# A decoder trunk with routed experts: router and shared gate as one product, choice of experts tile by tile, gate parts on GpSimd, and seventeen zero products at the start

## The chip, the core and the metric

The kernel runs on one core of a Trainium2 chip. The core has five engines with queues of their own: TensorE (PE, matrix products into the eight PSUM banks), VectorE (DVE), ScalarE (ACT), GpSimd (POOL, which works in SBUF) and SyncE (SP, which here issues nearly all DMA transfers). They wait for each other through semaphores. The metric is the device time of one execution in microseconds, lower is better.

## The reference

Two layers of a decoder on 256 tokens of 1024 values. In each, attention heads and four memory heads run side by side, one output projection and a layer norm follow, then a mixture of experts and a second norm. Everything is float32. What the change touches is the head of the mixture:

```
aff = jax.nn.sigmoid((xt @ w_router).astype(jnp.float32))          # 64 experts
sel = aff + router_bias
gscore = jnp.sum(lax.top_k(sel.reshape(n, 8, 8), 2)[0], axis=-1)    # 8 groups of 8
gidx = lax.top_k(gscore, 4)[1]
emask = jnp.repeat(gmask, 8, axis=1)
eidx = lax.top_k(jnp.where(emask, sel, -jnp.inf), 8)[1]
gates = jnp.take_along_axis(aff, eidx, axis=-1)
gates = gates / jnp.sum(gates, axis=-1, keepdims=True) * 2.5
...
h = jax.nn.silu(xb @ w_gate[e]) * (xb @ w_up[e]);  yb = h @ w_down[e]
shared = (jax.nn.silu(xt @ ws_gate) * (xt @ ws_up)) @ ws_down
```

Every expert has matrices of 1024x256, 1024x256 and 256x1024 (1 MB each), so the two layers read some 400 MB of expert weights.

## The kernel before

**Tiles.** The 256 tokens are two tiles of 128 (`t`). Products over the 1024 columns run over eight parts `k` of 128. A float32 product is two PE instructions in the trace, called rows below, so a product of one tile over eight parts is 16 rows. Weights stream from HBM through `ring`, twelve places of one matrix each; `first_place` says where the matrices of the dense part lie, `before_it` which load has to wait for which matrix in the same place. Some first expert weights are prefetched during the dense part, in the order that the SP block writes out.

**Start.** `warm(WARM)` multiplies zeros into bank 7 (L790, nine times) until the transposed input and the first half of the key weights are there; the first real product is L888.

**From the output projection to the experts**, per layer, in PE's order: the last rows of the projection (L869); the logits of tile 0 (L811, 64 columns a row); the shared expert's gate product of tile 0 (L1126, 256 columns), interrupted by products of zeros that open the output sums (L1153) and by the transposes of tile 1 (L800), which need its norm (DVE L1686 to L1693); logits of tile 1; the shared expert's other products; the rank product (place of each token within its expert, and counts), which waits for `chosen`; twelve more rows of the shared expert; then the gather of the tokens of eight experts into `xg` (L811, 32 rows), the first turn-back (L1222, with the product of the one-hot tile and `gparts`, the gates split into three bf16 parts) and the first gate product of the expert loop (L1250). The loop goes over 32 pairs of experts: gate (L1250), up (L1269), down (L1303), and scatter into the sums (L1311).

**DVE** in this stretch: norm of tile 1, two copies of its transpose to `xT`, then the choice for both tiles at once (L1853 to L1886: sigmoid's end, maxima of each group, comparison of the groups, eight best), `chosen`; the shared hidden product (L1891) of tile 0; rank, counts and the one-hot of eight experts (L1902); gates and their three parts (L1928 to L1939), with the shared hidden product of tile 1 among them; then copies of the gathered chunks. **ACT** takes square roots, makes the float32r copy of x (`x_high`), copies xT of tile 0, exponentiates the logits (L1567) and applies Silu to the shared gate products (L1570). **POOL** makes the low part of x of tile 1 (L774). **SP** issues weight loads, each behind a wait for the work that frees the place.

## Time and profile before

| | us |
|---|---|
| median of 3 runs | 1195.70 |
| the three runs | 1195.63, 1195.70, 1197.05 |
| the profiled execution, its own time | 1196.97 |
| its span from the first to the last instruction | 1195.2 |
| PE busy | 1154.6 (97%) |
| DVE, ACT, POOL busy | 345.4, 299.2, 54.9 |
| read from HBM | 445.91 MB |

The profile is of one execution. Times within it count from the start of the span. A view of lines tells the duration of one instruction, which for PE overlaps its neighbours; the chain of work tells start to start, so that a number of rows divided into it gives the pace. Busy slices and DMA shares are parts of each slice.

### The profile page before, as it was taken

How to read it: one execution, taken by the hardware profiler on the slowest of the kernel's cores; microseconds unless marked ns; L12 is line 12 of the kernel's file. 1: busy time of each engine (PE TensorE's matmuls, PEld its weight loads, DVE VectorE, ACT ScalarE, POOL GpSimd, SP SyncE). 2: the span in 40 equal slices, each digit the busy share in tenths (PEclk: the TensorE clock that was granted, in tenths of full speed). 3: DMA queues.
4: the chain of work that ended last, by engine and by line, in shares of the span. 5: the costliest groups of instructions: out<-in, count | busy, mean ns of one | idle time of the engine just before them, and what ended most of it. 6: DMA issues, size and time to landing. Idle time of an engine off the chain costs nothing.

```text
span 1195.2 us, 22277 instructions
## 1 busy us (share of the span) xinstructions
PE 1154.6 (97%) x8905; PEld 699.6 (59%) x8907; DVE 345.4 (29%) x900; ACT 299.2 (25%) x709; POOL 54.9 (5%) x90
## 2 busy tenths in 40 slices
PE   8999999999999999999999999999999999999995
PEld 6875755555555555554787658555555555555542
DVE  0335512222122212221523556122222222122214
ACT  1354212222122212121214523122221212122212
POOL 1341000000001000000011000000000010000000
PEclk9999999999999999999999999999999999999998
DMA  9944899999999999999980558999999999999994
GB/s 373 408 163 154 308 418 420 427 429 428 428 427 427 400 428 428 428 427 425 414 337 1 235 228 342 417 412 429 429 426 428 429 416 384 414 427 429 429 427 193
DMA packets 38374, 447.96 MB, mean 375 GB/s; under 512 B 4256, under 2 KB 4640, under 8 KB 9120
## 3 DMA queue, kind: packets, MB, share of 16 engines
q1 hardware_dynamic: 37584, 442.25, 88.8%
q10 hardware_dynamic: 720, 4.73, 1.0%
q8 instruction: 50, 0.82, 0.3%
q14 instruction: 20, 0.16, 0.0%
HBM read 445.91 MB, written 1.05 MB: 374 GB/s over the span
## 4 chain that ended last, share of the span: by engine, by line
PE 88%; DMA 8%; DVE 2%; issue 1%; ACT 1%; DVEq 0%; SPq 0%; ACTq 0%
PE bank L1250 18%; PE bank L1269 17%; PE bank L1303 17%; PE bank L811 8%; PE bank L830 8%; PE bank L1311 5%; PE bank L869 4%; DMA ring<-in_w_gate 4%; DMA ring<-in_w_down 3%; PE bank L1126 2%; PE bank L1276 2%; PE bank L845 1%; PE bank L1149 1%; PE bank L1025 1%; PE bank L888 1%
## 5 line engine op out<-in xcount | busy, mean ns | idle before, releaser
L1269 PE MATMUL bank<-ring,work 128*64 128x256 f32 x1952 | 225.0, 380 | 10.3 <-issue 10.3
L1250 PE MATMUL bank<-ring,work 128*64 128x256 f32 x1984 | 227.8, 382 | 4.9 <-DMA ring<-in_w_gate 4.7
L1303 PE MATMUL bank<-ring,work 128*32 128x512 f32 x1904 | 222.1, 595 | 0.2
L1250 PEld LDWEIGHTS bank<-ring,work 128*64 128x64 f32 x1984 | 137.9, 137 | 116.2 <-issue 41.9
L1269 PEld LDWEIGHTS bank<-ring,work 128*64 128x64 f32 x1952 | 145.1, 137 | 79.4 <-issue 14.7
L1965 DVE SCALAR_TENSOR_TENSOR yhalf<-bank,gcol,yhalf 128x512 fp32r<-128x512 f32 x124 | 93.1, 751 | 214.2 <-ACT yhalf L1591 214.2
L1591 ACT ACTIVATE yhalf<-bank,gcol 128x512 fp32r<-128x512 f32 x124 | 85.2, 687 | 181.3 <-PE bank L1303 181.3
L1957 DVE TENSOR_TENSOR work<-work,bank 128x256 f32<-128x256 f32 x64 | 26.9, 421 | 357.5 <-PE bank L1269 357.5
L1303 PEld LDWEIGHTS bank<-ring,work 128*32 128x32 f32 x1904 | 57.1, 110 | 117.2 <-issue 109.2
L1433 ACT ACTIVATE work<-bank 128x512 f32<-128x512 f32 (+4 forms) x177 | 77.9, 440 | 100.5 <-PE bank L811 41.8
L1433 ACT ACTIVATE back<-bank 128x128 fp32r<-128x128 bf16 x64 | 17.7, 277 | 276.2 <-PE bank L1222 276.2
L830 PE MATMUL bank<-xT,ring 128*128 128x256 f32 x352 | 77.7, 380 | 0.0
L811 PE MATMUL bank<-hot,xhalf 128*128 128x256 f32 x512 | 72.8, 293 | 4.7 <-DVE work L1672 4.3
L1311 PE MATMUL bank<-yhalf,back 64*128 64x512 f32 x504 | 75.7, 418 | 0.0
L1672 DVE COPY work<-bank 128x512 f32<-128x512 f32 (+3 forms) x77 | 51.3, 670 | 82.1 <-PE bank L811 48.8
L1581 ACT ACTIVATE work<-bank 128x256 f32<-128x256 f32 x64 | 24.6, 384 | 192.4 <-PE bank L1250 192.4
L830 PEld LDWEIGHTS bank<-xT,ring 128*128 128x128 f32 x352 | 66.3, 190 | 9.3 <-issue 0.7
L811 PEld LDWEIGHTS bank<-hot,xhalf 128*128 128x128 f32 x512 | 64.9, 190 | 10.7 <-DVE work L1672 7.2
L1311 PEld LDWEIGHTS bank<-yhalf,back 64*128 64x128 f32 x504 | 42.5, 185 | 30.1 <-issue 23.8
L869 PE MATMUL bank<-ring,work 128*128 128x512 f32 x128 | 57.8, 594 | 0.0
L869 PEld LDWEIGHTS bank<-ring,work 128*128 128x128 f32 x128 | 23.2, 190 | 23.3 <-issue 23.0
L782 POOL TENSOR_TENSOR x<-xhalf 128x1024 f32<-128x1024 f32 x4 | 9.5, 2414 | 510.9 <-PE bank L1303 510.9
(186 smaller groups left out, 825.3 us busy)
## 6 DMA issues: line engine op xcount, KB each, us to landing
ring<-in_w_gate SPq DMA_DIRECT2D x62, 2048.0 KB, 15.3
ring<-in_w_down SPq DMA_DIRECT2D x56, 2048.0 KB, 16.3
ring<-in_w_up SPq DMA_DIRECT2D x56, 2048.0 KB, 17.1
ring<-in_w_up SPq DMA_DIRECT2D x10, 1024.0 KB, 6.8
ring<-in_w_in_b SPq DMA_DIRECT2D x3, 3072.0 KB, 19.7
ring<-in_w_out SPq DMA_DIRECT2D x4, 2048.0 KB, 12.4
ring<-in_w_down SPq DMA_DIRECT2D x7, 1024.0 KB, 10.4
home<-in_w_gate SPq DMA_DIRECT2D x4, 1024.0 KB, 16.2
```

Source lines behind the costliest of these rows:

```text
L811: last = pe.matmul(dst, a, b, start=(n == 0), stop=(n == len(pairs) - 1))
L830: mm = pe.matmul(bank_at(g)[:, c * 256:(c + 1) * 256], w[:, k, c0 + c * P:c0 + (c + 1) * P], moving[:, k, :], start=(k == 0), stop=(k == K ...
L869: last = pe.matmul(bank_at(g)[:], mixT[:, c, t * P:(t + 1) * P], item_view((l, f"out{half}"), 512)[:, c, :], start=start, stop=(done == KT))
L1250: last = pe.matmul(gate_bank[slots_of(e), 0:HID], xg[:, k, slots_of(2 * j + e)], w[e][:, k, :], start=(k == 0), stop=(k == KT - 1))
L1269: last = pe.matmul(up_bank[slots_of(e), 0:HID], xg[:, k, slots_of(2 * j + e)], w[e][:, k, :], start=(k == 0), stop=(k == KT - 1))
L1303: last = pe.matmul(yb[half][rows_of(t, e), :], hT[b][:, f, slots_of(e, t)], w[e][:, f, half * 512:half * 512 + 512], start=(f == 0), stop= ...
L1311: pe.matmul(sums[2 * t + half][:], back[b][rows_of(t), :], yhalf[rows_of(t), n, half * 512:half * 512 + 512], start=False, stop=False)
L1433: return act.activation(dst, src, ACT.Copy)
L1591: act.activation(yhalf[:, 0, half * 512:half * 512 + 512], yb[half][:], ACT.Copy, scale=gcol[:, j:j + 1])\
L1672: return dve.tensor_copy(dst, src)
L1957: dve.tensor_tensor(hidrow, sg, up_bank[:, 0:HID], ALU.mult).then_inc(s_("h_ready"), 1)
L1965: dve.scalar_tensor_tensor(out=yhalf[:, 1, part], in0=yb[half][:], scalar=gcol[:, j:j + 1], in1=yhalf[:, 0, part].bitcast(F32), op0=ALU.mu ...
```

## The change

- `wr`, the router's weights, moves in front of the ring (`store` holds both), and the shared gate's weights are laid out on the host in four column blocks of 64, at ring place 0. So router and shared gate form one moving operand of 5 x 64 = 320 columns, `router_gate[:, :, k, :]`. For each tile one product of 320 columns (`logits_and_gate`) goes to one bank (3 for tile 0, 0 for tile 1). In layer 0 the shared weights swap their places and their turn in the loads with `out1`, as layer 1 had it.
- DVE chooses per tile (`choose(t)`), on 64 columns; the groups are masked by one addition instead of a product and an addition. ACT makes an exponential per tile and copies the second half of tile 1's xT.
- DVE makes the gate sums and their reciprocals; POOL scales the gates and splits them into the three parts (six steps, each waited for). PE waits for these steps through the semaphore `const`.
- The shared hidden product of tile 1 stands ahead of the gate sums. The gather's second and third chunk wait for one shared hidden product each.
- `WARM` is 17 instead of 9.

```
-         ("xr1", "DD", (0, 1)), ("logit", "A", (2,)), ("rank", "D", (2,))],
+         ("logit0", "A", (3,)), ("xr1", "DA", (0, 1)), ("logit1", "A", (0,)), ("rank", "D", (3,))],
...
-        {"in1": 0, "in0": 3, "memkv": 6, "out0": 8, "shared": 3, "out1": 0},
+        {"in1": 0, "in0": 3, "memkv": 6, "out0": 8, "out1": 3, "shared": 0},
...
-        ring = sb("ring", [P, 2 * REGION * MATRIX])
+        store = sb("store", [P, KT * NE + 2 * REGION * MATRIX])
+        wr = store[:, 0:KT * NE].rearrange("p (k n) -> p k n", k=KT)
+        ring = store[:, KT * NE:]
+        router_gate = store[:, 0:KT * (NE + HID)].rearrange("p (c k n) -> p c k n", k=KT, n=NE)
...
-        shared_gu = ((banks[3][:, 0:HID], banks[3][:, HID:2 * HID]), (banks[0][:, 0:HID], banks[1][:, 0:HID]))
+        shared_gate = (banks[3][:, NE:NE + HID], banks[0][:, NE:NE + HID])
+        shared_up = (banks[2][:, 0:HID], banks[1][:, 0:HID])
...
-        WARM = 9
+        WARM = 17
...
                 used(sp, (l, "out1"))
-                if l == 0:
-                    pair(0, 0, 1, 0)
-                else:
-                    expert(1, 0, 3, 1)
-                    expert(1, 0, 2, 2)
+                expert(l, 0, 3, 1)
+                expert(l, 0, 2, 2)
...
                 used(sp, (l, "shared"))
-                if l == 0:
-                    expert(0, 0, 3, 1)
-                    expert(0, 0, 2, 2)
-                else:
-                    pair(1, 0, 1, 0)
+                pair(l, 0, 1, 0)
...
+                pool.wait_ge(sem(f"gate_sums_{l}"), 1)
+                for t in range(TT):
+                    step(pool.tensor_scalar(gate[:, t, :], gate[:, t, :], grec[:, t:t + 1], None, ALU.mult))
+                gp = [gparts[:, :, :, i] for i in range(3)]
+                step(pool.tensor_copy(gp[0], gate[:]))
+                step(pool.tensor_tensor(gate[:], gate[:], gp[0], ALU.subtract))
+                step(pool.tensor_copy(gp[1], gate[:]))
+                step(pool.tensor_tensor(gp[2], gate[:], gp[1], ALU.subtract))
...
+                def logits_and_gate(t):
+
+                    g = G[l, f"logit{t}"]
+                    dst = bank_at(g)[:, 0:NE + HID].rearrange("p (c n) -> p c n", n=NE)
+                    bank_free(pe, g)
+                    for k in range(KT):
+                        if k % 4 == 0:
+                            evacuated(pe, G[l, f"xr{t}"] + k // 4)
+                        last = pe.matmul(dst, xT[:, k, t * P:(t + 1) * P], router_gate[:, :, k, :], start=(k == 0), stop=(k == KT - 1))
+                    last.then_inc(sem("group"), 1)
...
-                pe.wait_ge(sem("chosen"), l + 1)
+                pe.wait_ge(sem("chosen"), TT * (l + 1))
                 g = G[l, "rank"]
                 bank_free(pe, g)
-                bank = bank_at(g)
+                pe.wait_ge(sem(f"shared_silu_{l}"), 1)
...
-                        if backs is None and k == 2:
-                            pe.wait_ge(sem(f"shared_h_{l}"), TT)
+                        if backs is None and k in (1, 2):
+                            pe.wait_ge(sem(f"shared_h_{l}"), k)
...
-                    pe.wait_ge(s_("gates_set"), 1)
+                    pe.wait_ge(sem("const"), CONSTS + (GATE_STEPS + 1) * l + GATE_STEPS)
...
                 norm_std(2 * l, 1)
+                logit_exp(0)
+                turned_x(1, 1)
                 x_high(1)
-                g = G[l, "logit"]
-                filled(act, g)
-                act.activation(rsc[:], bank_of(g, TT, NE), ACT.Exp, scale=-1.0).then_inc(read, 1)
+                logit_exp(1)
...
+                def choose(t):
...
+                    link(dve.tensor_reduce(grank[:, t, :], cmp1[:, t], AX_X, ALU.add))
+                    link(dve.tensor_scalar(goff[:, t, :], grank[:, t, :], float(TOPK_GROUPS), -BIG, ALU.is_ge, ALU.mult))
+                    grouped = sel[:, t, :].rearrange("p (g e) -> p g e", g=NGROUP)
+                    link(dve.tensor_tensor(grouped, grouped, to_rows(goff[:, t, :], PER_GROUP), ALU.add))
+                    link(dve.max(top8[:, t, :], sel[:, t, :]))
+                    link(dve.match_replace(rsc[:, t, :], top8[:, t, :], sel[:, t, :], -2.0 * BIG))
+                    dve.tensor_tensor(chosen[:, t, :], rsc[:, t, :], sel[:, t, :], ALU.not_equal).then_inc(sem("chosen"), 1)
...
+                shared_hidden(1)
                 link(dve.tensor_tensor(gate[:], aff[:], chosen[:], ALU.mult))
                 link(dve.tensor_reduce(gsum[:], gate[:], AX_X, ALU.add))
-                link(dve.reciprocal(grec[:], gsum[:]))
-                for t in range(TT):
-                    last = dve.tensor_scalar(gate[:, t, :], gate[:, t, :], grec[:, t:t + 1], ROUTED_SCALE, ALU.mult, ALU.mult)
-                shared_hidden(1)
-                link(last)
-                gp = [gparts[:, :, :, i] for i in range(3)]
-                link(copy(gp[0], gate[:]))
-                link(dve.tensor_tensor(gate[:], gate[:], gp[0], ALU.subtract))
-                link(copy(gp[1], gate[:]))
-                dve.tensor_tensor(gp[2], gate[:], gp[1], ALU.subtract).then_inc(s_("gates_set"), 1)
+                link(dve.tensor_scalar(gsum[:], gsum[:], 1.0 / ROUTED_SCALE, None, ALU.mult))
+                dve.reciprocal(grec[:], gsum[:]).then_inc(sem(f"gate_sums_{l}"), 1)
```

PE's instructions in layer 0 from the end of the output projection on, before (a program's product counts once here; `ident` is the identity for transposes, `zeros` the products that open sums):

```order
L869 MATMUL bank5<-ring,work 128x512 x2
L811 MATMUL bank2<-wr,xT 128x64 x8
L1126 MATMUL bank3<-ring,xT 128x256 x6
L1153 MATMUL bank4<-zeros 128x512
L1153 MATMUL bank6<-zeros 128x512
L800 MATMUL bank0<-ident,x 128x128 x4
L800 MATMUL bank1<-ident,x 128x128 x4
L1126 MATMUL bank3<-ring,xT 128x256 x2
L1153 MATMUL bank5<-zeros 128x512
L1153 MATMUL bank7<-zeros 128x512
L811 MATMUL bank2<-wr,xT 128x64 x8
L1126 MATMUL bank3<-ring,xT 128x256 x8
```

The same place in the change:

```order
L872 MATMUL bank5<-store,work 128x512 x2
L1141 MATMUL bank3<-store,xT 128x320 x8
L1162 MATMUL bank4<-zeros 128x512
L1162 MATMUL bank6<-zeros 128x512
L803 MATMUL bank0<-ident,x 128x128 x4
L803 MATMUL bank1<-ident,x 128x128 x4
L1162 MATMUL bank5<-zeros 128x512
L1162 MATMUL bank7<-zeros 128x512
L1141 MATMUL bank0<-store,xT 128x320 x8
L1129 MATMUL bank2<-store,xT 128x256 x8
L1129 MATMUL bank1<-store,xT 128x256 x2
L814 MATMUL bank3<-chosen,before 128x128
```

Nothing of the gate product is left behind the transposes of tile 1, and ten products of the shared up matrix stand ahead of the rank product.

DVE before, from the one-hot of the first eight experts to the last gate part (`route` holds gates and affinities, `work` the shared hidden values):

```order
L1902 TENSOR_TENSOR hot8_51<-slot_no,rank 128x512
L1927 TENSOR_LOAD nround_i
L1927 ISA x2
L1928 TENSOR_TENSOR route<-route,chosen 128x128
L1929 TENSOR_REDUCE gsum<-route 128x2
L1930 RECIPROCAL grec<-gsum 128x2
L1932 TENSOR_SCALAR route<-route,grec 128x64 x2
L1891 TENSOR_TENSOR work<-work,bank1 128x256
L1672 CAST gparts<-route 128x128
L1937 TENSOR_TENSOR route<-route,gparts 128x128
L1672 CAST gparts<-route 128x128
L1939 TENSOR_TENSOR gparts<-route,gparts 128x128
```

DVE in the change, from the same one-hot:

```order
L1905 TENSOR_TENSOR hot8_51<-slot_no,rank 128x512
L1932 TENSOR_LOAD nround_i
L1932 ISA x2
L1894 TENSOR_TENSOR work<-work,bank1 128x256
L1934 TENSOR_TENSOR route<-route,chosen 128x128
L1935 TENSOR_REDUCE gsum<-route 128x2
L1936 TENSOR_SCALAR gsum<-gsum 128x2
L1937 RECIPROCAL grec<-gsum 128x2
```

And POOL in the change, between the low part of x and its next wait for the loop:

```order
L769 TENSOR_TENSOR xhalf<-x,xhalf 128x1024
L773 TENSOR_SCALAR route<-route,grec 128x64 x2
L775 CAST gparts<-route 128x128
L776 TENSOR_TENSOR route<-route,gparts 128x128
L777 CAST gparts<-route 128x128
L778 TENSOR_TENSOR gparts<-route,gparts 128x128
```

The six steps behind the reciprocal have gone from DVE to POOL, and the shared hidden product has gone ahead of the gate sums.

## Rows read from the trace of the kernel before

**Rows 1.** The page, busy totals and DMA share in 40 slices:

```profile
PE 1154.6 (97%) x8905; PEld 699.6 (59%) x8907; DVE 345.4 (29%) x900; ACT 299.2 (25%) x709; POOL 54.9 (5%) x90
...
DMA  9944899999999999999980558999999999999994
```

**Rows 2.** Waits of PE: line, releaser, total us, times, longest:

```profile
PE bank L1269 <- issue: 10.3, 8, 1.3
PE bank L1250 <- DMA ring<-in_w_gate: 4.7, 6, 0.9
```

**Rows 3.** Chain of work, layer 0: start, us, what:

```profile
114.38 1.73 PE bank L811 x16
...
123.14 7.83 PE bank L1126 x36
130.97 0.13 PE bank L811 x2
...
138.61 3.67 PE bank L1250 x32
```

**Rows 4.** Timeline of PE, layer 0, with idle time before in brackets:

```profile
135.03 3.19 PE L811 MATMUL bank<-hot,xhalf 128*128 128x256 f32 x24 [0.21 <-DVE work L1891]
138.37 0.17 PE L811 MATMUL bank<-gparts,hot_tile 128*128 128x12 bf16 x1 [0.15 <-issue]
```

**Rows 5.** Chain of work, layer 1:

```profile
715.45 1.73 PE bank L811 x16
...
739.44 3.67 PE bank L1250 x32
```

**Rows 6.** Stretch 132:134 (last columns: clock, DMA share, GB/s), and SP's issues:

```profile
132.00:134.00 2.00, 2.00 (x11) 1.56 (x11) 1.54 (x6) 0.00 (x0) 0.00 (x0) 1.00 0.00 0
...
133.76 0.33 SPq L448 DMA_DIRECT2D ring<-in_w_up  x1
...
142.31 0.33 SPq L455 DMA_DIRECT2D ring<-in_w_gate  x1
```

**Rows 7.** Start: timeline, then L888 by starting time (ns min/median/max, first to last start):

```profile
1.26 4.02 PE L790 MATMUL bank<-zeros 128*128 128x512 bf16 x9 [1.26 <-DVE zeros L1699]
7.24 10.44 PE L888 MATMUL bank<-xT,ring 128*128 128x256 f32 x32 [1.96 <-DMA ring<-in_w_in_a]
10.13 0.33 SPq L423 DMA_DIRECT2D ring<-in_w_in_a  x1
...
L888 PE MATMUL bank<-xT,ring x4: 633/634/688, 10.9 to 12.3; 128*64 128x256 f32 x4
...
L888 PE MATMUL bank<-xT,ring x6: 379/380/483, 13.5 to 14.8; 128*128 128x256 f32 x5, 128*64 128x256 f32 x1
```

**Rows 8.** Timeline of DVE, layer 0, from the norm to the choice:

```profile
117.63 1.28 DVE L1693 SCALAR_TENSOR_TENSOR x<-x,rstd,lnrow 128x1024 f32<-128x1024 f32 x1
...
123.57 0.49 DVE L1853 TENSOR_SCALAR route<-route 128x128 f32<-128x128 f32 x1 [2.46 <-ACT route L1567]
...
125.08 0.29 DVE L1855 TENSOR_TENSOR route<-route,biasrow 128x128 f32<-128x128 f32 x1
125.41 1.19 DVE L1859 MAX8 top<-route 128x8 f32<-128x8 f32 x16
...
130.32 0.29 DVE L1886 TENSOR_TENSOR chosen<-route 128x128 bf16<-128x128 f32 x1
```

**Rows 9.** POOL's groups by form (busy us, mean ns), then its timeline:

```profile
L770 POOL TENSOR_SCALAR soft<-acc,rden 128x256 f32<-128x256 f32 x18 | 16.4, 923 | 47.6 <-DVE rden L1781 47.6
L770 POOL TENSOR_SCALAR soft<-acc,rden 128x128 f32<-128x128 f32 x12 | 7.2, 602 | 34.6 <-DVE rden L1781 34.6
L774 POOL TENSOR_TENSOR xhalf<-x,xhalf 128x1024 fp32r<-128x1024 f32 x2 | 5.7, 2846 | 115.4 <-ACT xhalf L1433 115.4
...
1.60 0.29 POOL L709 CAST ident_bf<-ident 128x128 bf16<-128x128 f32 x1
1.95 0.20 POOL L710 MEMSET ones<- 128x128 bf16 x1
```

More of the change, by code:

```diff
@@ L1880, in _ @@
[L1880 to L1886 removed]
+                    link(last)
+                    link(dve.tensor_tensor(gsc[:, t, :], top2[:, t, :, 0], top2[:, t, :, 1], ALU.add))
```

130 lines of the change are left out of this document (55 added, 75 removed).

## The prediction

> **What bounds the kernel now.** I read the page's totals and slices first. TensorE (PE) is busy 97% of the span, and the DMA engines stand at nine or ten tenths in most slices [rows 1]. So two resources are near their limit, and the question for each stage is which waits for which. The table of waits answers it: over 1195 us PE waited only 4.7 us for expert weights and 10.3 us for "issue" inside L1269, in stretches of 1.3 us at most [rows 2]. Apart from that PE simply works from one instruction to the next.
>
> The stretch that the change rewrites runs, in layer 0, from the end of the output projection at 114.38, where the logits begin, to the first gate product of the experts at 138.61. The chain of work is there PE all the way down to the rank product at 130.97 [rows 3], and in those 24.23 us PE idled 0.21 us ahead of the gather's third chunk and 0.15 ahead of the first turn-back [rows 4]. Layer 1 takes 739.44 - 715.45 = 23.99 us [rows 5]. So time taken off PE here is time off the path, as long as the helpers keep up.
>
> Does a shorter stretch shorten the expert loop, where DMA runs at its limit? The DMA share is 0.00 from 132 to 134: the queue was empty, because SP waited for the shared expert's products before it could issue at 133.76, and for the first expert gate product before it issued at 142.31 [rows 6]. Both releases come from PE. Whatever PE gains before them, the weight stream starts that much earlier, and the loop, paced by that stream or by PE, moves as a block.
>
> At the start there are nine products of zeros from 1.26 us, and the first real product (L888) starts at 7.24, when its weights have landed. Its 32 instructions take 10.44 us. Those that start up to 12.3 us last 634 ns, those after 13.5 us 379 [rows 7]. At one level of the clock (2.4 GHz) 32 instructions at 0.215 us would take 6.9 us. The excess is 3.5 us, of which some 2.8 are clock: from 7.24 to about 12.85 PE ran at the lower level (1.2 GHz), and half of those 5.6 us is lost. The granted-clock column itself says 1.00 there; the durations are what I go by.
>
> **The change part by part.**
>
> (a) *One product of 320 columns.* Before, each tile costs 16 rows of 64 columns (1.73 us, 0.108 each) and 16 rows of 256 (36 rows in 7.83, so 0.215 without the joints) [rows 3]. 64 columns are a quarter of 256 but cost half: the stationary load sets the pace. In the change a row has 320 columns: 0.215 x 320/256 = 0.269, so 4.30 us a tile against 1.73 + 3.44 = 5.17. That is 0.87 us a tile, 1.74 a layer, all of it on the path.
>
> (b) *The new order on PE*, layer 0, from 114.38: product of tile 0 to 118.68; two zero products (0.43) to 119.11. The transposes of tile 1 need the second norm, which ends at 117.63 + 1.28 = 118.91 [rows 8], so they don't wait. Transposes 0.93 to 120.04 and zeros to 120.47. The first half of xT is copied by DVE as before (0.65 us after its half, 120.3); the second half is now ScalarE's (ACT), one copy of 0.55 by about 120.7, needed only at the fifth row. Tile 1 to 124.77. Twenty rows of the shared up product to 129.07.
>
> (c) *Choice tile by tile.* Before, DVE chose for both tiles from 123.57 to 130.61 (7.04 us), and PE got to the rank product at 130.97: hidden by 0.36 us [rows 3, 8]. In the change each operation is half as wide. A 128-wide one lasts 0.29 us and 0.04 to the next; of that about half is independent of the width, so 64 columns take 0.22. The reciprocal (the 1.0 us between the first step and 125.08) and the maxima (sixteen in 1.19) halve; one step of two is gone where the group mask was made and applied. Going through the list: about 4.5 us a tile, 9.0 in all against 7.04. But tile 0 can start early: its logits are ready at 118.68, ACT's exponential at 119.0, and DVE is free behind its copy at about 120.7. So tile 0 ends at 125.2; tile 1's exponential is out at 125.1; tile 1 ends at 129.7. PE, there at 129.07, waits 0.65 us. Queued behind that wait are the rank product, 12 up rows and the gather. The bounds: no wait, if each step costs 8% less; 1.5 us, if halving the width saved nothing outside the two large steps.
>
> (d) *From the rank product to the gates.* Rank product to 129.86; 12 up rows (2.58) to 132.44; DVE's path from the rank product to the one-hot isn't touched; before, it was done while PE worked off those 12 rows, and it still is. Gather 32 rows at 0.133 (24 rows in 3.19 [rows 4]) to 136.69. The shared hidden product of tile 1 now stands ahead of the gate sums, and waits for the up rows (132.5 to 133.0); the third chunk of the gather needs it at 133.5. No wait, where there were 0.21 us before.
>
> (e) *Gate parts on GpSimd (POOL).* DVE is left with a product, a sum (0.33 each), a scaling and a reciprocal of two columns (0.2 each): 1.0 us, done at 134.0. Then six steps on POOL, each waited for: two scalings 128x64, two casts and two subtractions 128x128. POOL's scaling lasts 602 ns at 128 columns and 923 at 256, so 2.5 ns a column and 0.44 us at 64; a cast of 128x128 lasted 290 ns, and the next step began 0.06 later; a 1024-wide subtraction 2846 ns, from which I take 0.55 us at 128 [rows 9]. Sum 0.88 + 0.59 + 1.10 + 6 x 0.07 = 3.0 us, so the parts are ready at 137.05. On DVE the same steps ended at 136.2, and nobody waited. PE needs them at 136.69 for the first turn-back: it waits 0.35 us. Behind that wait stands the whole expert loop. With 0.24 us for turning back, the first gate product starts at 137.3 instead of 138.61. **Gain 1.3 us a layer, 2.6 us for both.** Bounds: 1.8 a layer if neither wait (c) nor (e) appears; nothing if POOL needs 4.3 us (rows of 0.65 on average: the 128-wide scaling is already 0.60).
>
> The Trainium skill, GPSIMD Engine Reference, section 4.1 Engine selection, tells to keep elementwise work on VectorE: about twice as slow on GpSimd with two inputs, about equal with one. The trace has one input at 2.5 ns a column on POOL, so it doesn't bear out the "equal". By the page's ratios, applied to DVE's rows, the six steps would take an estimated 2.8 us, 0.2 less than my sum.
>
> (f) *ACT and POOL moved.* The exponential and the half copy of xT go ahead of ACT's copy of x for tile 1, which could start at 118.9 and now starts at 120.7; POOL's low part (2.85 us [rows 9]) ends at 125.7 instead of 124.0. The gather needs it at 132.4, SP's load into x waits for it: 1 MB issued 1.7 us later while 2 MB are under way. Hidden; if that cover were gone it would cost 1.7 us of DMA.
>
> (g) *Layer 0's loads.* out1 and the shared weights change places and order. The bytes are the same. The second pair's gate weights now wait for the shared products; issued at 132.5 into an empty queue, some 7 us before they have landed, they are needed after the gate and up products of the first pair, at about 145. Zero; layer 1 has this order already, and its whole stretch is the shorter one.
>
> (h) *Seventeen zero products.* At the lower level each takes 0.427 us (nine in 4.02 with the last one's tail [rows 7]), so they'd end at 1.26 + 17 x 0.427 = 8.5, 1.3 us after the real product could start. If the clock rises while they run, they end earlier and the real product finds 2.4 GHz. In the trace it rose after 5.6 us of unbroken work. The same after 1.26 is 6.9: 13 zeros slow, 4 fast, PE free at 7.75, 0.5 late. Gain 2.8 - 0.5 = **2.3 us**. The second half of the weights isn't in the way: SP saw it landed at 10.13 [rows 7], and it is wanted at 11.2. Bounds: 2.8 (the rise comes early enough) and -1.3 (zeros leave the clock low). The dense part behind it never waits for data, so this is carried to the end.
>
> **Sum.** The profiled execution took 1196.97 (span 1195.2 and 1.8 around it): 1196.97 - 2.6 - 2.3 = 1192.1. It is 1.3 us above the median of 1195.7; the runs fall at 1195.6, 1195.7 and 1197.05. If that 1.3 is the moment when the clock rises, a typical run has less to win at the start, and 1192 stays; if it is elsewhere, 1190.8. I say **1191.4**.
>
> **The rivals.** *No wait at all* (the choice and POOL both faster than I sized them): 2 x 1.8 + 2.8 = 6.4 off, less half of the 1.3: 1189.9. For it: each wait is a few tenths. *POOL sets the gates*: the interleaved bf16 writes cost more than any POOL row shows, six steps take 4.3 us, routing gains nothing: 1194.0. *The weight stream hides it*: PE comes earlier to the experts but the bytes set the end; then only part of (h) survives, 1194.5. Against it stands the empty queue [rows 6]. *Zeros don't lift the clock*: +1.3 - 2.6 gives 1195.0; for it speaks that nine zeros (4 us) were followed by a slow product. *Slower than before*, by the same place as the second: from 5.5 us for POOL's six steps on, the kernel loses more at both turn-backs than it wins elsewhere; at 7.5 us (1.6 us for each of the four 128-wide steps) each layer starts its experts 3.1 us later than now, +6.3 - 2.3: about 1199. No row of POOL is near that: 7.5 us is 2.5 times my sum.
>
> **Chances.** Forecast 0.55, no waits 0.13, POOL sets the gates 0.13, weight stream 0.05, zeros without effect 0.10, slower 0.04. A measurement of this kernel can tell about 0.2% (2.4 us) from no change, so faster means under 1193.3: forecast and no waits, and a part of the second and third: 0.78. Same 0.18, slower 0.04. The range takes in the bounds of (c), (e) and (h) down to 1189.0 and reaches to the POOL and stream cases up to 1194.6.
>
> **What would show it.** L888 at 379 ns from its first instruction, starting at 7.2 to 7.8 (else (h) fails). The 320-column rows 0.27 apart; if they are 0.32 (the sum of the two old rows), (a) gives nothing. PE's wait for `chosen` 0 to 1.5 us. POOL's six steps 3 us, ending within 0.5 of the gather's end. First gate product of layer 0 at 137.3 less the gain of the start, and the same shift still there at the last product. If the shift at the first gate product is right and missing at the end, the weight stream was the bound.

## The result, and the profile of the changed kernel

The changed kernel takes 1197.65 us (median of 20 runs, 1196.03 to 1200.59) against 1196.05 for the kernel before, run beside it (20 runs, 1194.73 to 1197.87). The ratio is 1.0015, with a 95% interval of 1.001 to 1.0021: slightly slower, where 1191.4 was forecast. The profiled execution took 1200.59 (span 1198.9), 3.6 us more than the profiled execution of before. The totals and the DMA shares of the page stand nearly where they stood in [rows 1]:

```profile
PE 1153.4 (96%) x8849; PEld 695.0 (58%) x8851; DVE 349.0 (29%) x908; ACT 300.2 (25%) x713; POOL 60.2 (5%) x102
...
DMA  9935799999999999999970657999999999999995
```

So the time moved inside stretches. I read them in the order of the prediction. The start, from the timeline of PE (start, us, what; idle time before it in brackets), against [rows 7]:

```profile
1.26 5.33 PE L793 MATMUL bank<-zeros 128*128 128x512 bf16 x17 [1.26 <-DVE zeros L1707]
7.56 4.68 PE L891 MATMUL bank<-xT,store 128*128 128x256 f32 x19 [0.97 <-DMA store<-in_w_in_a]
```

And the same line's instructions by their durations (ns min/median/max, first to last start):

```profile
L891 PE MATMUL bank<-xT,store x32: 379/379/483, 7.6 to 14.8; 128*128 128x256 f32 x16, 128*64 128x256 f32 x16
```

All 32 real products run at 379 ns, the higher level of the clock (2.4 GHz), from the first one on. The output projection ends at 111.88 instead of 114.38: 2.5 us won. Then layer 0's stretch, again PE's timeline, with the weight loads (PEld) of the second wide product as its first row, against [rows 3, 4]:

```profile
118.03 4.07 PEld L1141 LDWEIGHTS bank<-store,xT 128*128 128x128 f32 x16 [0.46 <-DVE xT L1680]
118.06 4.54 PE L1141 MATMUL bank<-store,xT 128*128 128x320 f32 x16
122.44 4.48 PE L1129 MATMUL bank<-store,xT 128*128 128x256 f32 x20
129.28 0.22 PE L814 MATMUL bank<-chosen,before 128*128 128x128 bf16 x1 [2.36 <-issue]
...
129.39 4.25 PE L1129 MATMUL bank<-store,xT 128*128 128x256 f32 x12
133.08 4.60 PE L814 MATMUL bank<-hot,xhalf 128*128 128x256 f32 x32
138.54 0.17 PE L814 MATMUL bank<-gparts,hot_tile 128*128 128x12 bf16 x1 [0.87 <-DVE work L1680]
...
138.78 1.52 PE L1254 MATMUL bank<-store,work 128*64 128x256 f32 x12
```

PE stands idle for 2.36 us ahead of the rank product, the twelve up rows behind it need 4.25 us, and there is a second wait of 0.87 ahead of the turn-back. In the chain of work the wide product of tile 0 takes 4.31 us and that of tile 1 4.54: its first weight load waited 0.46 us for DVE's copy of xT. The first gate product starts at 138.78, where it started at 138.61: all that the start had won is gone. From 111.88 the stretch takes 26.90 us instead of 24.23. Layer 1, from the chain of work, against [rows 5]:

```profile
716.24 4.31 PE bank L1141 x16
...
726.97 4.32 PE bank L1129 x20
733.64 0.27 PE bank L814 x2
733.91 4.27 PE bank L1129 x12
...
743.07 0.17 PE bank L814
```

With the turning back behind the last row (0.24 us, as in layer 0) that is 743.31 - 716.24 = 27.07 us instead of 23.99. The account from trace to trace: start -2.5, layer 0 +2.67, between the stretches +0.6, layer 1 +3.08, the rest -0.2; together +3.7, which is the difference of the spans.

Why is the choice late? The timelines of DVE (the first three rows) and of POOL (the others), layer 0:

```profile
120.28 0.23 DVE L1878 TENSOR_TENSOR cmp<-cmp,lower 128x64 f32<-128x64 f32 x1
120.54 2.75 DVE L1879 TENSOR_TENSOR cmp<-cmp 128x64 f32<-128x64 f32 x1
123.33 0.22 DVE L1880 TENSOR_REDUCE grank<-cmp 128x8 f32<-128x64 f32 x1
```

```profile
120.30 2.92 POOL L769 TENSOR_TENSOR xhalf<-x,xhalf 128x1024 fp32r<-128x1024 f32 x1 [27.60 <-ACT xhalf L1437]
135.20 0.98 POOL L773 TENSOR_SCALAR route<-route,grec 128x64 f32<-128x64 f32 x2 [11.98 <-DVE grec L1937]
...
137.73 0.46 POOL L778 TENSOR_TENSOR gparts<-route,gparts 128x128 bf16<-128x128 f32 x1
```

One comparison (L1879, an addition of two 64-wide inputs) lasts 2.75 us, its neighbours 0.22. It ends at 123.29, and POOL's low part of x ends at 123.22. In layer 1 the same line lasts 2.76 us. Nothing in the two instructions depends on the other. And the clock, from the table of stretches (busy us of PE, PEld, DVE, ACT, POOL, then granted clock, DMA share, GB/s):

```profile
126.00:128.00 2.00, 0.92 (x5) 0.47 (x3) 1.79 (x15) 0.00 (x0) 0.00 (x0) 1.00 0.74 311
128.00:130.00 2.00, 0.72 (x5) 0.70 (x6) 1.79 (x9) 0.00 (x0) 0.00 (x0) 1.00 0.00 0
130.00:132.00 2.00, 2.00 (x8) 1.66 (x7) 1.42 (x7) 0.00 (x0) 0.00 (x0) 0.65 0.00 0
132.00:134.00 2.00, 2.00 (x7) 1.64 (x7) 0.25 (x1) 0.00 (x0) 0.00 (x0) 0.50 0.00 0
134.00:136.00 2.00, 2.00 (x19) 2.00 (x18) 1.90 (x8) 1.20 (x2) 0.71 (x2) 1.00 0.72 156
```

PE goes back to work at 129.28. The granted clock is still 1.00 up to 130, its mean is 0.65 from 130 to 132 and 0.50, the lower level (1.2 GHz), from 132 to 134: by these means it fell at about 130.6 (an estimate), 1.3 us behind the end of the idle time. That is the cause of the up rows' 4.25 us, 2.81 at the full clock (the same twelve rows in the runs below).

### The profile page after: what moved, and what is told of

The parts are those of the page before. It is cut to its first block, busy times and chain, and to the rows that moved or that the text cites. A ratio compares the mean times of both kernels' runs of the same rounds, so it can differ in the third digit from the quotient of the medians.

```text
span 1198.9 us, 22189 instructions
## 1 busy us (share of the span) xinstructions
PE 1153.4 (96%) x8849; PEld 695.0 (58%) x8851; DVE 349.0 (29%) x908; ACT 300.2 (25%) x713; POOL 60.2 (5%) x102
## 4 chain that ended last, share of the span: by engine, by line
PE 88%; DMA 8%; DVE 2%; issue 1%; ACT 1%; DVEq 0%; SPq 0%; ACTq 0%
PE bank L1254 17%; PE bank L1273 17%; PE bank L1307 17%; PE bank L814 8%; PE bank L833 8%; PE bank L1315 5%; PE bank L872 4%; DMA store<-in_w_gate 4%; DMA store<-in_w_down 3%; PE bank L1280 2%; PE bank L1141 1%; PE bank L1129 1%; PE bank L848 1%; PE bank L1158 1%; PE bank L1028 1%
## 5 line engine op out<-in xcount | busy, mean ns | idle before, releaser
L1273 PE MATMUL bank<-store,work 128*64 128x256 f32 x1952 | 225.2, 380 | 10.4 <-issue 10.3
L1254 PE MATMUL bank<-store,work 128*64 128x256 f32 x1984 | 227.8, 382 | 5.1 <-DMA store<-in_w_gate 5.1
L1307 PE MATMUL bank<-store,work 128*32 128x512 f32 x1904 | 222.0, 595 | 0.2
L1254 PEld LDWEIGHTS bank<-store,work 128*64 128x64 f32 x1984 | 138.0, 137 | 116.4 <-issue 41.9
L1273 PEld LDWEIGHTS bank<-store,work 128*64 128x64 f32 x1952 | 145.9, 137 | 79.2 <-issue 15.6
L1307 PEld LDWEIGHTS bank<-store,work 128*32 128x32 f32 x1904 | 57.1, 110 | 117.1 <-issue 109.1
L833 PE MATMUL bank<-xT,store 128*128 128x256 f32 x352 | 77.7, 380 | 0.0
L1680 DVE COPY work<-bank 128x512 f32<-128x512 f32 (+3 forms) x77 | 51.6, 672 | 80.2 <-PE bank L814 49.6
L833 PEld LDWEIGHTS bank<-xT,store 128*128 128x128 f32 x352 | 66.5, 190 | 9.2 <-issue 0.7
L872 PE MATMUL bank<-store,work 128*128 128x512 f32 x128 | 57.8, 594 | 0.0
L872 PEld LDWEIGHTS bank<-store,work 128*128 128x128 f32 x128 | 23.2, 191 | 23.3 <-issue 23.0
```

What stands on the lines that cost most here:

```text
L833: mm = pe.matmul(bank_at(g)[:, c * 256:(c + 1) * 256], w[:, k, c0 + c * P:c0 + (c + 1) * P], moving[:, k, :], start=(k == 0), stop=(k == K ...
L872: last = pe.matmul(bank_at(g)[:], mixT[:, c, t * P:(t + 1) * P], item_view((l, f"out{half}"), 512)[:, c, :], start=start, stop=(done == KT))
L1254: last = pe.matmul(gate_bank[slots_of(e), 0:HID], xg[:, k, slots_of(2 * j + e)], w[e][:, k, :], start=(k == 0), stop=(k == KT - 1))
L1273: last = pe.matmul(up_bank[slots_of(e), 0:HID], xg[:, k, slots_of(2 * j + e)], w[e][:, k, :], start=(k == 0), stop=(k == KT - 1))
L1307: last = pe.matmul(yb[half][rows_of(t, e), :], hT[b][:, f, slots_of(e, t)], w[e][:, f, half * 512:half * 512 + 512], start=(f == 0), stop= ...
L1680: return dve.tensor_copy(dst, src)
```

## The experiments

**Theory 1**: POOL's low part of tile 1 holds DVE. While a POOL instruction on SBUF runs, a DVE instruction that takes two inputs from SBUF doesn't end before it. The change brought this about from both sides. Counted from the start of the stretch, the choice starts 3.1 us earlier than before (at 6.05 instead of 9.19), and the low part, behind ACT's copy of x, 1.7 us later (at 8.42 instead of 6.75). **Theory 2**: the idle time costs a second time, through the clock. **Theory 3**: the gate parts on POOL make PE wait at the turn-back. The rivals are named with each run: the choice is long by itself, the wide product or the new order costs what was lost, the zeros don't last to the end.

**The zeros alone**, in the kernel before:

```diff
-        WARM = 9
+        WARM = 17
```

> The kernel before with seventeen zero products instead of nine, nothing else. Theory: in the changed kernel's trace the first real product ran at the full clock from its first instruction and the end of the output projection came 2.5 us earlier (111.88 against 114.38); nothing later takes it back, so this kernel is 1.5 to 2.8 us faster than before (ratio 0.9977 to 0.9988). Rival: the weight stream sets the end and takes the start's gain back: ratio 1.000.

Measured: 1193.80 us (11 runs), ratio 0.9991 (0.9982 to 1.0). PE's timeline at the start and at the first turn-back:

```profile
7.21 5.11 PE L888 MATMUL bank<-xT,ring 128*128 128x256 f32 x21
...
135.50 0.17 PE L811 MATMUL bank<-gparts,hot_tile 128*128 128x12 bf16 x1 [0.17 <-issue]
```

The first turn-back stands 2.87 us earlier than before in the trace [rows 4], and the routing stretches are as long as ever (24.2 and 24.0 us). At the end the medians lie 2.0 apart (1195.79 to 1193.80), inside the 1.5 to 2.8 expected; the ratio makes the gain 1.1 us, less than expected, and its interval just reaches no gain. So step (h) holds in the trace, and at the end something between 1 and 2 us of it is seen.

**The rest alone**: the changed kernel with nine zeros.

```diff
-        WARM = 17
+        WARM = 9
```

> The changed kernel with nine zero products. Theory (the routing part costs 2.7 us in layer 0 and 3.1 in layer 1): 4 to 6 us slower than before. Rival (the seventeen zeros are to blame, for instance through the clock later on): not slower than before.

Measured: 1198.09 us (10 runs), ratio 1.0022 (1.0009 to 1.0035). The direction is the expected one; the size, 2.3 us over before, is below the 4 to 6 expected, and only 0.4 over the changed kernel itself. The trace shows the same stretches as above (27.12 and 27.10 us, PE idle 2.35 us ahead of the rank product; the turn-back comes 1.73 us later than in the changed kernel). Its start:

```profile
7.42 9.27 PE L891 MATMUL bank<-xT,store 128*128 128x256 f32 x32 [2.20 <-DMA store<-in_w_in_a]
```

These 32 rows took 10.44 us before [rows 7], so with nine zeros too this execution reached the stretch 1.0 us earlier than before (113.39). That is a part of what is missing. The rest isn't settled: its ten executions spread over 6 us (1195.26 to 1201.14), with mean clocks from 0.992 to 0.996.

**Taking the low part away from the choice**: POOL computes 8 columns of it instead of 1024.

```diff
+                 pool.wait_ge(sem("normed"), 4 * l + 1)
+                 pool.memset(xhalf[:, 1, t, :].bitcast(F32), 0.0).then_inc(sem("low_zero"), 1)
...
-                pool.tensor_tensor(by_chunk(xhalf[:, 1, t, :]), by_column(x[:, t, :]), by_chunk(xhalf[:, 0, t, :].bitcast(F32)),
+                pool.tensor_tensor(xhalf[:, 1, t, 0:8], x[:, t, 0:KT * 8:KT], xhalf[:, 0, t, 0:8].bitcast(F32),
```

> The changed kernel, but GpSimd's subtraction of 1024 columns per partition (the low part of x for tile 1) covers 8 columns; the rest is set to zero by GpSimd some 15 us earlier. So the low part of tile 1 is left out of the gather and of x. Theory 1 (a two-input instruction of VectorE waits while GpSimd runs its own two-input one): the 2.75 us instruction at the comparison of groups lasts 0.23, the choice ends 2.5 us earlier, TensorE idles under 0.7 us at the rank product and keeps its clock; the first gate product of layer 0 starts at about 134.8 instead of 138.78, and the kernel is 6 to 8 us faster than the changed one, 4 to 6 faster than before (about 1191). Rival (the long instruction has a cause of its own, not GpSimd): the instruction still lasts 2.7 us and the time is that of the changed kernel.

Measured: 1191.57 us (7 runs), ratio 0.9969 (0.9958 to 0.9979). Timelines of POOL, DVE and PE, layer 0:

```profile
120.03 0.20 POOL L772 TENSOR_TENSOR xhalf<-x,xhalf 128x8 fp32r<-128x8 f32 x1 [12.42 <-ACT xhalf L1440]
...
134.07 0.46 POOL L781 TENSOR_TENSOR gparts<-route,gparts 128x128 bf16<-128x128 f32 x1
...
120.21 0.23 DVE L1882 TENSOR_TENSOR cmp<-cmp 128x64 f32<-128x64 f32 x1
...
127.06 0.22 PE L817 MATMUL bank<-chosen,before 128*128 128x128 bf16 x1 [0.47 <-issue]
...
134.88 0.17 PE L817 MATMUL bank<-gparts,hot_tile 128*128 128x12 bf16 x1 [0.91 <-DVE work L1683]
```

The comparison is back at 0.23, the wait at 0.47, the clock doesn't fall, and 6.1 us are gone from the median (this run is 4.2 us under the kernel before, run beside it, the changed kernel was 1.6 over). That excludes a choice that is long by itself, and it leaves no room for a loss by the wide product or by the order on PE: the stretches are 23.60 and 23.59 us, shorter than before. The time is near the forecast of 1191.4, but in part by luck: the stretches gain 0.63 and 0.40 us, where 1.3 each was forecast.

**Filling the idle time**: ten zero products into an open sum, ahead of the wait, so that PE is busy and nothing else changes (the trace has records of nine).

```diff
+                for n in range(10):
+                    pe.matmul(sums[3][:], zeros[:, 0:P], zeros[:], start=False, stop=False)
```

> The changed kernel with ten products of zeros, added to an open sum, in the place where TensorE waits for the choice (10 x 0.215 us against a wait of 2.36). The choice itself is as late as before. Theory 2 (after 2.4 us of idling the clock went to its lower level, 1.2 GHz, and the 12 up rows took 4.1 us instead of 2.6, and a few more rows behind them): with the wait filled the rows behind the rank product run at 0.215 us each, 1.5 us less in layer 0 and 1.5 to 1.9 in layer 1, the kernel 2 to 3.4 us faster than the changed one. Rival (the rows are slow for another reason, such as the bank or the weights' address): the rows stay slow and the time stays.

Measured: 1197.34 us (12 runs, 1195.13 to 1198.12), ratio 1.0011 (1.0002 to 1.002). PE's timeline, and the stretch behind it from the table of stretches:

```profile
126.63 2.32 PE L1178 MATMUL bank<-zeros 128*128 128x512 bf16 x9
129.13 0.22 PE L814 MATMUL bank<-chosen,before 128*128 128x128 bf16 x1 [0.18 <-issue]
...
129.24 2.81 PE L1129 MATMUL bank<-store,xT 128*128 128x256 f32 x12
```

```profile
132.00:134.00 2.00, 2.00 (x18) 2.00 (x18) 1.74 (x7) 0.95 (x2) 0.40 (x1) 1.00 0.75 131
```

In the trace theory 2 holds: the granted clock stays at 1.00, the twelve rows need 2.81 us, and the two stretches are 25.43 us each, 1.5 and 1.6 shorter than in the changed kernel. In the time it isn't shown: the median gained only 0.3 of the 2 to 3.4 expected, and beside the kernel before this run is 1.55 us over, the changed kernel 1.60. The mean granted clock that each execution lists gives a hint. Of the changed kernel's 20 executions four stood at 0.993 and took 1199.2 us on average, and five at 0.996, with 1197.0; with the fill all twelve stood at 0.996 or 0.997, with 1196.7. So it may be that the fill takes away what a lower clock costs, and that most executions hadn't much of that. This is an inference: a mean doesn't tell where the clock was low, and the kernel before, whose trace has no such wait, also ranges from 0.994 to 0.997. What is shown is the trace: the drop costs about 1.5 us a layer where it happens, as in both layers of the profiled execution, which was one of the four.

**The collision, made in the kernel before**: ACT exponentiates before it copies x for tile 1, so that POOL's low part falls into the choice there too.

```diff
-                x_high(1)
                 g = G[l, "logit"]
                 filled(act, g)
                 act.activation(rsc[:], bank_of(g, TT, NE), ACT.Exp, scale=-1.0).then_inc(read, 1)
+                x_high(1)
```

> The kernel before, with one change: ScalarE exponentiates the logits before it copies x of tile 1, so that GpSimd's subtraction of 1024 columns falls into VectorE's choice of experts (about 125.7 to 128.6) instead of ahead of it. Theory 1 (VectorE's two-input instructions are held while GpSimd's two-input one runs): one instruction of the comparison of groups lasts 2 to 2.7 us instead of 0.29, chosen comes about 2 us later, TensorE idles 1.6 to 2.2 us at the rank product; 3 to 7 us slower than before over both layers (the upper end if the clock drops as well). Rival (the choice is slow only in the changed kernel's per-tile form): no long instruction, time within 1 us of before.

Measured: 1198.08 us (10 runs) against 1196.26 of before, ratio 1.002 (1.0009 to 1.0031): slower, as expected, but by 1.8 us (2.4 by the ratio) and not by 3 to 7. Timelines of POOL, DVE and PE, layer 0:

```profile
125.82 2.85 POOL L774 TENSOR_TENSOR xhalf<-x,xhalf 128x1024 fp32r<-128x1024 f32 x1 [30.31 <-ACT xhalf L1433]
...
125.46 1.19 DVE L1859 MAX8 top<-route 128x8 f32<-128x8 f32 x16
126.68 2.03 DVE L1861 TENSOR_TENSOR gsc<-top 128x16 f32<-128x16 f32 x1
...
132.61 0.22 PE L811 MATMUL bank<-chosen,before 128*128 128x128 bf16 x1 [1.32 <-issue]
```

Another line is hit, a sum of 16 columns: 2.03 us instead of 0.19, until 128.71; POOL ends at 128.67. The sixteen MAX8, one input each, run under POOL at their usual pace. PE waits 1.32 us where it didn't wait at all; the clock stays at 1.00. The layers' stretches are 1.5 and 1.6 us longer. So POOL's instruction, moved into the choice, makes a loss of the same kind without the rest of the change; it is smaller, since the hold is shorter and the clock stays up.

**Giving DVE one input from PSUM**: the changed kernel, where tile 0's scores and one of the two comparison matrices lie in a free PSUM bank, so that no DVE instruction of that choice that falls under POOL's low part has two inputs from SBUF; POOL's low part stays where it is. PE waits for tile 0's choice before it writes into that bank.

```diff
+                pe.wait_ge(sem("chosen"), TT * l + 1)
...
+                    sel_t, two = (banks[2][:, n * NE:(n + 1) * NE] for n in range(2))
...
-                    link(dve.tensor_tensor(sel[:, t, :], aff[:, t, :], biasrow[:, l, :], ALU.add))
+                    link(dve.tensor_tensor(sel_t, aff[:, t, :], biasrow[:, l, :], ALU.add))
...
-                    link(dve.tensor_tensor(cmp1[:, t], cmp1[:, t], cmp2[:, t], ALU.add))
+                    link(dve.tensor_tensor(cmp1[:, t], cmp1[:, t], cube(two), ALU.add))
```

> The changed kernel; for tile 0 the selection scores and one matrix of comparisons lie in PSUM bank 2, so that no instruction of that choice reads two inputs from SBUF once GpSimd's subtraction has begun (TensorE waits for the first choice before it uses the bank). Theory 1 in the form 'what is held is an instruction that needs VectorE's second read of SBUF': the first choice is not held and ends at about 122.1 instead of 124.9; the second one's first step (one input, SBUF to SBUF) may be held until GpSimd ends at 123.2, as L1853 of before, 0.49 us long, was; chosen at about 127.6 instead of 129.2, idle at the rank product about 1 us, clock kept; 3.5 to 6 us faster than the changed kernel (1191.7 to 1194). Rival (GpSimd holds every VectorE instruction, or its writes): the held instruction moves elsewhere, time of the changed kernel.

Measured: 1191.62 us (6 runs, 1190.81 to 1191.90), ratio 0.9962 (0.9948 to 0.9977). Timelines of POOL and of DVE, then of PE:

```profile
120.32 2.85 POOL L769 TENSOR_TENSOR xhalf<-x,xhalf 128x1024 fp32r<-128x1024 f32 x1 [27.58 <-ACT xhalf L1438]
...
120.64 0.22 DVE L1885 TENSOR_TENSOR cmp<-cmp,bank 128x64 f32<-128x64 f32 x1
...
122.93 0.29 DVE L1869 TENSOR_SCALAR route<-route 128x64 f32<-128x64 f32 x1 [0.49 <-ACT route L1571]
...
127.53 0.22 PE L814 MATMUL bank<-chosen,before 128*128 128x128 bf16 x1 [0.46 <-issue]
```

Instructions with two inputs, one of them in PSUM, run for 0.22 us in the middle of POOL's 2.85, and POOL isn't slower either. Only L1869, a scaling with its one input and its output in SBUF, is stretched, to 0.29 us from 0.19, until 123.22, just over POOL's end (123.17). That is the strongest sign for theory 1: same time, same work, other memory, 6.0 us off the changed kernel, at the upper end of the 3.5 to 6 expected. Beside the kernel before it is 4.6 us under.

**Gate sums first**: the same, with the gate sums ahead of the shared hidden product of tile 1, so that POOL can start earlier.

```diff
-                shared_hidden(1)
                 link(dve.tensor_tensor(gate[:], aff[:], chosen[:], ALU.mult))
...
+                shared_hidden(1)
```

> c_psum, and the gate sums stand ahead of the shared hidden product of tile 1, in VectorE's idle time behind the one-hot. Theory 3 (TensorE's 0.9 us ahead of the first turn-back is the wait for GpSimd's six steps, which end at 134.53 in the run with the short subtraction while TensorE goes on at 134.88): the steps start about 1 us earlier, the wait goes; 0.6 to 0.9 us less a layer, 1.2 to 1.8 us faster than c_psum. Rival (the wait is for VectorE's copies of gathered chunks, which end within 0.2 us of it): no gain.

Measured: 1190.59 us (6 runs), ratio 0.9955 (0.994 to 0.997), the fastest of all. Timelines of POOL (first and last step) and of PE:

```profile
130.86 0.98 POOL L773 TENSOR_SCALAR route<-route,grec 128x64 f32<-128x64 f32 x2 [8.05 <-DVE grec L1942]
...
133.39 0.48 POOL L778 TENSOR_TENSOR gparts<-route,gparts 128x128 bf16<-128x128 f32 x1
...
134.29 0.17 PE L814 MATMUL bank<-gparts,hot_tile 128*128 128x12 bf16 x1
```

The wait at the turn-back, 0.92 us with the sums behind, is gone. So theory 3 holds, though the profile put that wait down to DVE's copy of the gather (L1680): DVE's last such copy ends here at 135.00, behind the turn-back, which didn't wait for it. The other traces say the same. In all seven kernels with the parts on POOL and the sums behind, in both layers, the turn-back starts 0.34 to 0.38 us after POOL's last step ends (138.19 to 138.54 in the changed kernel, 134.53 to 134.88 with the short low part), while its distance from the end of DVE's copy goes from 0.13 to 0.37. The stretches are 22.99 and 22.71 us, 1.24 and 1.28 shorter than before and together 1.6 shorter than with the sums behind; the median gained 1.0 of the 1.2 to 1.8 expected.

**Gate parts back on DVE**, from the kernel with PSUM, in the old order:

```diff
-                    step(pool.tensor_scalar(gate[:, t, :], gate[:, t, :], grec[:, t:t + 1], None, ALU.mult))
...
+                    last = dve.tensor_scalar(gate[:, t, :], gate[:, t, :], grec[:, t:t + 1], ROUTED_SCALE, ALU.mult, ALU.mult)
```

> c_psum with the gate parts back on VectorE, in the order of before (sums, scaling, shared hidden product, parts). It undoes the move to GpSimd. Theory 3: GpSimd's parts cost a wait of 0.9 us a layer, VectorE's none of that but later copies of the chunks, 0.15 us in the kernel before; so 0.5 to 1.5 us faster than c_psum. Rival: the parts on VectorE delay the copies by more than they save; not faster.

Measured: 1191.34 us (6 runs), ratio 0.996 (0.9945 to 0.9974). PE waits 0.17 us at the turn-back and 0.22 inside the gather; the stretches are 23.44 and 23.18, against 23.67 and 23.65 with the parts on POOL in the order of the change. In these traces, then, moving the gate parts to GpSimd as the change does it wins nothing; it does only with the sums put ahead. The times don't settle it: the medians (1191.62, 1191.34, 1190.59) are in that order, but their intervals overlap, and the 0.3 us between the first two is below the 0.5 to 1.5 expected.

Two more runs ask what in POOL's instruction holds DVE. **One input instead of two**, a copy of x in the place of the low part, which this kernel leaves out:

```diff
-                pool.tensor_tensor(by_chunk(xhalf[:, 1, t, :]), by_column(x[:, t, :]), by_chunk(xhalf[:, 0, t, :].bitcast(F32)),
-                                   ALU.subtract).then_inc(sem("xlo"), 1)
+                pool.tensor_copy(by_chunk(xhalf[:, 1, t, :]), by_column(x[:, t, :])).then_inc(sem("xlo"), 1)
```

> The changed kernel, with GpSimd's low part of tile 1 replaced by a plain copy of x (one input instead of two; the low part is left out of the result, so the sums of tile 1 are of other values). Theory 1, as it stands: only an instruction with two inputs from SBUF holds VectorE's, so the comparisons of tile 0 take 0.23 us each in place of one of 2.75, GpSimd's copy itself lasts something near 2.6 us (1024 columns by the 2.5 ns of a column that its one-input steps of 64 columns show), TensorE's wait ahead of the rank product is about 0.5 us and the time is 1191.6, as with the low part shortened. Rival: any long GpSimd instruction on SBUF holds them; then a VectorE instruction lasts as long as what is left of the copy, the wait stays above 2 us and the time stays near 1197.

Measured: 1193.63 us (10 runs) against 1195.36 of before, ratio 0.9983 (0.9972 to 0.9994). Timelines of POOL, DVE, PE:

```profile
119.99 2.03 POOL L769 CAST xhalf<-x 128x1024 fp32r<-128x1024 f32 x1 [27.57 <-ACT xhalf L1436]
...
120.00 2.11 DVE L1877 TENSOR_TENSOR cmp<-cmp,lower 128x64 f32<-128x64 f32 x1
...
128.34 0.22 PE L813 MATMUL bank<-chosen,before 128*128 128x128 bf16 x1 [1.70 <-issue]
```

Theory 1 as I had put it before this run fell: a POOL instruction with one input holds DVE just as well, for as long as it lasts (2.11 us). The time falls between the two expectations: that copy is shorter, PE waits 1.70 us instead of 2.36, and the clock stays at 1.00. Whether POOL's instruction has one input or two didn't matter here.

**The low part in eight pieces** of 128 columns:

```diff
...
+                for k in range(KT):
+                    if k == KT - 1:
+                        pool.wait_ge(sem("low_piece"), (KT - 1) * (l + 1))
+                    piece = pool.tensor_tensor(low[:, k], full[:, k], high[:, k], ALU.subtract)
+                    piece.then_inc(sem("xlo" if k == KT - 1 else "low_piece"), 1)
```

> The changed kernel, with GpSimd's low part of tile 1 as eight instructions of 128 columns, one behind the other, in place of one of 1024. If a VectorE instruction is held only until the GpSimd instruction that runs ends, each of the two-input VectorE instructions under the low part is stretched by at most one piece (about 0.4 us), three or four of them in turn: the chosen experts of tile 1 are there 1 to 2 us earlier than in the changed kernel, TensorE waits 0.5 to 1.5 us ahead of the rank product, the clock stays up, and the time is 1191.5 to 1194. Rival: whoever holds the shared way keeps it while the next piece is already queued; then one VectorE instruction again lasts about 2.8 to 3.2 us, and the time is 1197 to 1198.

Measured: 1193.15 us (10 runs), ratio 0.9981 (0.9966 to 0.9995). Timelines of POOL, DVE, PE:

```profile
119.98 4.02 POOL L774 TENSOR_TENSOR xhalf<-x,xhalf 128x128 fp32r<-128x128 f32 x8 [27.60 <-ACT xhalf L1442]
...
120.22 0.42 DVE L1884 TENSOR_TENSOR cmp<-cmp 128x64 f32<-128x64 f32 x1
...
121.14 0.46 DVE L1888 TENSOR_TENSOR route<-route,goff 128x64 f32<-128x64 f32 x1
...
122.58 0.41 DVE L1868 TENSOR_SCALAR route<-route 128x64 f32<-128x64 f32 x1
...
127.54 0.22 PE L819 MATMUL bank<-chosen,before 128*128 128x128 bf16 x1 [0.94 <-issue]
```

The hold lasts for one instruction at a time. DVE's four two-input steps under the pieces last 0.33 to 0.47 us, none 2.75, although POOL works 4.02 us instead of 2.85. The next piece in the queue doesn't keep the way closed. The scaling L1868, with one input, is stretched as well, to 0.41 us from 0.19; the maxima, the sum over columns and the reciprocal, one input each too, keep their pace.

## Why the prediction was wrong

**Right.** (h): 2.3 us forecast, 2.5 in the trace, 2.0 in the medians of the kernel with the zeros alone (1.1 by its ratio). The size came out nearer than its path: the zeros took 5.33 us and not the 6.5 of the sum, so that PE was free at 6.59, and what it waited for until 7.56 was its weights. (a): 4.31 us for sixteen 320-column rows, 4.30 forecast; tile 1's need 4.54, behind the wait for xT that (b) had at nothing. (g): PE waited for no weights between 138.6 and 175, as before. (e), POOL's six steps: 135.20 to 138.19, so 3.0 us as forecast. The expert loop moved with its start: between the stretches and behind them the traces differ by 0.6 and 0.2 us. The Trainium skill's ratios (GPSIMD Engine Reference, section 4.1 Engine selection) had given an estimate of 2.8 for POOL's steps.

**The step that failed is (f), the line "Hidden; if that cover were gone it would cost 1.7 us of DMA", and through it (c).** I asked who waits for POOL's low part, found the gather and SP, both far off, and gave it no price. I didn't ask what runs beside it. In layer 0 it had stood at 121.13 to 123.98, where DVE waited for the exponential; in the change it stands at 120.30, in the choice of tile 0. Most of that is (c)'s own doing, which brought the choice forward by 3.1 us onto the low part. The bounds of (c), no wait to 1.5 us, had only widths and overheads in them. Measured were 2.36 and 2.36; without the hold, 0.45 to 0.48 in four kernels, inside the bounds and next to the 0.65 forecast.

The sign was in the rows on record. L1853 of before, a scaling with one input, lasted 0.49 us at 123.57 [rows 8], though 128-wide instructions around it lasted 0.29 (and itself 0.23 in the run where POOL came later): it ended at 124.06, and POOL's low part ended at 123.98. I used that row as the start of the list and not as a row that is too long. The Trainium skill has the rule as well: SBUF — State Buffer, section "Who interferes with whom", says that VectorE and GpSimd share a port pair as an exclusive lock, that a VectorE instruction with two SBUF inputs contends with a GpSimd instruction that reads SBUF, and that one with at most one SBUF input doesn't, outside the two-port modes. The runs agree: 2.75 us for two SBUF inputs, 0.22 with one of the two in PSUM. The scaling with one input was held too (0.49 us instead of 0.23 before, 0.29 and 0.41 instead of 0.19 in the kernels with PSUM and with the pieces); whether it ran in a two-port mode no trace shows. I had looked up the price of work on GpSimd in the skill and not its neighbours.

**A term was missing: the clock behind the wait.** The sum took each wait at its own length. After waits of 0.46 to 1.70 us the granted clock stayed at 1.00 in the profiled executions; after 2.36, and after 2.35 in the kernel with nine zeros, it fell to 0.50 in both layers, and the twelve rows cost 1.4 us more (4.08 from start to start instead of 2.65). Layer 0's 4.0 us between forecast (-1.3) and trace (+2.67), by the chain of work, are: 1.7 of longer wait, 1.6 for the rank product and the up rows (4.35 instead of 2.72; 1.4 of it is the clock), 0.5 of longer wait at the turn-back, 0.2 for tile 1's wide product and 0.1 for the transposes, less 0.2 for a gather that was quicker than its sum (4.05 instead of 4.25); together 3.9, and 4.0 before rounding.

**A term was too small: (e) on the path.** POOL's steps start 1.56 us behind the last up row (133.64 to 135.20), just as in the sum (132.44 to 134.0), and last the 3.0 us of the sum. Two terms behind them were off. The sum let PE go on as POOL's last step ends, and by the profile's ends there are 0.34 to 0.38 us more. And the gather, which covers POOL's steps, takes 3.8 to 4.05 us and not 4.25. So PE's wait was 0.87 to 1.11 us where 0.35 was forecast, in all kernels with this order, the slow clock or not. What fills the 0.35 us no run shows. Two such waits are most of what the kernel with the short low part lacks of the forecast's gain.

The rivals: the slower case put the loss at the turn-back, where PE did wait, but 0.87 us and not for slow steps, which it wanted at 7.5 us; the longer wait, 2.36 us, stood ahead of the rank product. None of them had engines hold each other up without a semaphore.

**What stays open.** Between the kernel with the fill and the one with PSUM the two stretches account for 3.5 us, the medians for 5.7. The expert loops of the fill's profiled execution are 3 us longer; a wait of 1.1 us for a down weight stands in its table of waits and in none of the others'. Over the twelve traces the part from the first gate product of layer 0 to the stretch of layer 1 takes 576.5 to 579.0 us, and the part behind layer 1's stretch 453.8 to 457.2. That the loops vary so from execution to execution is seen, why isn't. How much of the changed kernel's median is the clock is open too.

## What to carry to other kernels

When a change moves an instruction of GpSimd, lay it beside VectorE's timeline at its new place: in these runs a VectorE instruction there with two inputs from SBUF lasted until its end, with no semaphore in between, and so did a scaling with one input. Put one operand in PSUM, cut the GpSimd instruction in pieces, or move it to where VectorE waits anyway. And when an instruction's duration in a trace doesn't fit its width, find what ended at the same moment before using its row.

## What the runs showed of the hardware

- A GpSimd instruction with one input holds VectorE as one with two does: 2.11 us under a copy of 2.03, 2.75 under a subtraction of 2.92. No effect the other way is clear: POOL's 1024-wide subtraction took 2.92 us while it held DVE in the changed kernel, but 2.85 while it held DVE for 2.03 us in the kernel with the collision made, and 2.85 where it held nothing for long.
- The hold is by instruction: eight pieces give 0.33 to 0.47 us a VectorE step, one gives 2.75.
- A VectorE scaling (TENSOR_SCALAR, float32, one input and the output in SBUF) is held as well: 0.49 us instead of 0.23 at 128 columns, 0.41 instead of 0.19 at 64. Maxima, sums over columns (TENSOR_REDUCE) and a reciprocal under POOL's instructions were not.
- TensorE goes on 0.34 to 0.38 us after the end that the profile gives GpSimd's last step, in fourteen places.
- Eight GpSimd subtractions of 128 columns take 4.02 us, one of 1024 takes 2.85: about 0.17 us for each further instruction. That is an estimate: the last piece waits for the seven before it, and DVE's steps fall between them.
- Four executions of one kernel at a mean clock of 0.993 took 2.2 us more than five at 0.996. That a drop of the clock after a wait doesn't come in each execution is inferred from this, not shown.
